# The first norm's inputs, factors and splits, re-ordered in a two-block model kernel

## What is computed

```python
def rms_norm(x, g):
    xf = x.astype(jnp.float32)
    y = xf * lax.rsqrt(jnp.mean(xf * xf, axis=-1, keepdims=True) + EPS)
    return (y * g.astype(jnp.float32)).astype(x.dtype)

def swiglu(x, w_gu, w_down):
    gate, up = jnp.split(x @ w_gu, 2, axis=-1)
    return (jax.nn.silu(gate) * up) @ w_down
```

## Time and profile before

| | us |
|---|---|
| median of 3 runs | 1676.66 |
| lowest and highest | 1675.67, 1677.74 |
| span of the profiled execution | 1677.2 |
| TensorE busy | 1640.7 (98%) |
| VectorE busy | 1189.8 (71%) |
| ScalarE busy | 878.0 (52%) |
| GpSimd busy | 51.2 (3%) |

### The profile page before, as it was taken

The page is one execution under the profiler, slowest core; times in us unless marked ns, Lnnn a source line. Parts: engine busy times, 40 slices in busy tenths (PEclk is TensorE's granted clock), DMA queues, the critical chain, the costliest instruction groups (busy, mean ns, idle before and its releaser), DMA issues.

```text
span 1677.2 us, 24153 instructions
## 1 busy us (share of the span) xinstructions
PE 1640.7 (98%) x9644; PEld 1425.4 (85%) x9644; DVE 1189.8 (71%) x1991; ACT 878.0 (52%) x1521; POOL 51.2 (3%) x87
## 2 busy tenths in 40 slices
PE   8999999999999999999999999999999999999997
PEld 7888899778888888889888888888888998888886
DVE  6766658957666776675877676786667887676777
ACT  5544456755444444455755444655444666454445
POOL 0000000001000000001210000000000000000000
PEclk9999999999999999999999999999999999999999
DMA  9545356034555455545345555545554443565541
GB/s 368 193 186 190 137 188 240 5 135 176 188 188 189 176 204 190 194 160 223 141 171 204 192 193 180 216 184 188 188 189 182 151 145 126 198 222 189 189 163 50
DMA packets 32111, 301.54 MB, mean 180 GB/s; under 512 B 3824, under 2 KB 4352, under 8 KB 6016
## 3 DMA queue, kind: packets, MB, share of 16 engines
q1 hardware_dynamic: 32000, 300.01, 48.6%
HBM read 298.93 MB, written 1.06 MB: 179 GB/s over the span
## 4 chain that ended last, share of the span: by engine, by line
PE 87%; DVE 7%; ACT 3%; issue 1%; POOL 0%; DMA 0%; SPq 0%; DVEq 0%; ACTq 0%
PE bank L477 28%; PE bank L467 27%; PE bank L466 12%; PE bank L456 9%; PE bank L469 2%; DVE w_lo L429 1%; PE bank L507 1%; PE bank L2087 1%; PE bank L580 1%; DVE x L848 1%; PE bank L581 1%; PE bank L605 1%; PE bank L2089 1%; PE bank L584 1%; PE bank L1684 1%
## 5 line engine op out<-in xcount | busy, mean ns | idle before, releaser
L429 DVE TENSOR_TENSOR w_lo<-w_raw,w_hi 128x1024 fp32r<-128x1024 f32 (+4 forms) x539 | 586.9, 1139 | 190.8 <-ACT w_hi L422 190.3
L467 PE MATMUL bank<-xT,w_hi 128*128 128x512 f32 x1920 | 673.8, 396 | 0.3 <-DVE w_lo L429 0.3
L422 ACT ACTIVATE w_hi<-w_raw 128x1024 fp32r<-128x1024 f32 (+5 forms) x543 | 500.3, 981 | 98.0 <-PE bank L477 82.1
L466 PE MATMUL bank<-xT,w_lo 128*128 128x256 f32 x1680 | 468.4, 279 | 0.0
L467 PEld LDWEIGHTS bank<-xT,w_hi 128*128 128x128 f32 x1920 | 351.6, 188 | 69.9 <-DVE w_lo L429 0.5
L466 PEld LDWEIGHTS bank<-xT,w_lo 128*128 128x128 f32 x1680 | 316.7, 189 | 10.4
L795 ACT ACTIVATE ff_silu<-ff_silu 128x256 f32<-128x256 f32 x124 | 51.9, 418 | 387.8 <-DVE ff_silu L948 387.8
L477 PE MATMUL bank<-w_hi,hT_hi 128*128 128x512 f32 x480 | 187.5, 391 | 0.0
L477 PE MATMUL bank<-w_hi,hT_lo 128*128 128x512 f32 x480 | 186.8, 389 | 0.0
L477 PE MATMUL bank<-w_lo,hT_hi 128*128 128x512 f32 x480 | 186.8, 389 | 0.0
L948 DVE TENSOR_REDUCE ff_silu<-bank 128x256 f32<-128x512 f32 x124 | 85.7, 691 | 101.7 <-PE bank L467 100.6
(11 more groups left out here) (398 smaller groups left out, 2170.4 us busy)
## 6 DMA issues: line engine op xcount, KB each, us to landing
w_raw<-in_ffn_a SPq DMA_DIRECT2D x22, 1536.0 KB, 6.6
w_raw<-in_ffn_b SPq DMA_DIRECT2D x22, 1536.0 KB, 6.4
w_raw<-in_ffn_c SPq DMA_DIRECT2D x22, 1536.0 KB, 6.5
w_raw<-in_ffn_d SPq DMA_DIRECT2D x22, 1536.0 KB, 6.6
w_raw<-in_ffn_e SPq DMA_DIRECT2D x22, 1536.0 KB, 6.5
w_raw<-in_ffn_f SPq DMA_DIRECT2D x22, 1536.0 KB, 6.4
gains<-in_gains SPq DMA_DIRECT2D x11, 1024.0 KB, 5.0
w_raw<-in_mla_up SPq DMA_DIRECT2D x8, 1280.0 KB, 5.8
```

The source lines that it names most:

```text
L422: nc.scalar.activation(hi, src, ACTF.Copy).then_inc(w_hi_made, 1)
L429: nc.vector.tensor_tensor(lo, src, hi.bitcast(F32), ALU.subtract).then_inc(w_lo_made, 1)
L466: nc.tensor.matmul(o[:, 0:SEQ], lo[:, c], xT[:, k, 0, :], start=False, stop=False)
L467: ins = nc.tensor.matmul(o, hi[:, c], xT[:, k, :, :], start=(k == 0), stop=(k == KD - 1))
```

## The change

- SP issues token block 0 first, then the identity, then the factors as one row on one partition (4 KB in place of 512 KB). Token block 1 is issued by ACT, as its first instruction.
- A row of 128 ones is written by POOL. TensorE multiplies it with the factor row, two fp32 products of 512 columns into PSUM banks 0 and 1 (`pe_spread_gains`), as the first thing on TensorE and so ahead of the 12 warming matmuls. `dve_rms_apply` reads the factors of this norm from PSUM.
- The first weight chunk comes in two transfers, 1024 columns with a semaphore of its own, and the other 2048.
- DVE does all four applications ahead of splits and low parts. ACT puts a split between turn 0 and turn 1. The low part of piece 3 goes from DVE to POOL, between the two roots of norm 0 and norm 1.

```diff
-        by_pool = 4 if (name, i) == ("ffn_b", 0) else 0
+        by_pool = {("ffn_a", 0): (3,), ("ffn_b", 0): (0, 1, 2, 3)}.get((name, i), ())
...
+            if i == 0 and b <= GU // 2:
+                act.wait_ge(w_front_landed, 16)
+            else:
+                act.wait_ge(w_landed[c.slot], c.landed)
...
+        def pe_spread_gains():
+
+            pe.wait_ge(ones_row_made, 1)
+            pe.wait_ge(gains_landed, 16)
+            for half in range(2):
+                ins = nc.tensor.matmul(psum[half][:, :], ones_row, gains[0:1, half_of(half)], start=True, stop=True)
+            ins.then_inc(gains_spread, 1)
...
-            dve.wait_ge(gains_landed, 16 * (n + 1))
+            gain = gains[:, c]
+            if n == 0:
+                dve.wait_ge(gains_spread, 1)
+                gain = psum[c.start // 512][:, :]
+            else:
+                dve.wait_ge(gains_landed, 16 * (n + 1))
             dve.wait_ge(rooted, 2 * n + b + 1)
...
             apply(0, 1, half_of(0))
-            dve_low(0, 0)
             apply(0, 0, half_of(1))
-            dve_low(0, 1)
             apply(0, 1, half_of(1))
             dve_split(first["ffn_a"], 0, 2)
+            dve_low(0, 0)
+            dve_low(0, 1)
+            dve_split(first["ffn_a"], 2, 3)
             dve_low(0, 2)
-            dve_split(first["ffn_a"], 2, 4)
             dve_low(0, 3)
...
+                at = 0
+                if i == 0:
+                    at = GU // 2
+                    nc.sync.dma_start(raw[c.slot][:, 0:at], c.source[:, 0:at]).then_inc(w_front_landed, 16)
+                nc.sync.dma_start(raw[c.slot][:, at:c.cols], c.source[:, at:c.cols]).then_inc(w_landed[c.slot], 16)
...
+            nc.sync.dma_start(x[:, 0, :], t["x"][tok_of(0), :]).then_inc(x_landed[0], 16)
             nc.sync.dma_start(const[:, 0:P], t["const"][:, 0:P]).then_inc(ident_landed, 16)
-            for b in range(TB):
-                nc.sync.dma_start(x[:, b, :], t["x"][tok_of(b), :]).then_inc(x_landed[b], 16)
-            nc.sync.dma_start(gains[:, 0:D], t["gains"][0:1, 0:D].to_broadcast([P, D])).then_inc(gains_landed, 16)
+            nc.sync.dma_start(gains[0:1, 0:D], t["gains"][0:1, 0:D]).then_inc(gains_landed, 16)
...
         def pe_program():
+            pe_spread_gains()
             pe.wait_ge(ident_landed, 16)
...
         def act_program():
+            nc.scalar.dma_start(x[:, 1, :], t["x"][tok_of(1), :]).then_inc(x_landed[1], 16)
             act_squares(0, x, False)
-            act_turn(0, (0, 1))
-            act_split(first["ffn_a"], 0, 2)
+            act_turn(0, (0,))
+            act_split(first["ffn_a"], 0, 1)
+            act_turn(0, (1,))
+            act_split(first["ffn_a"], 1, 2)
             act_turn(0, (2,))
...
         def pool_program():
+            nc.gpsimd.memset(ones_row, 1.0).then_inc(ones_row_made, 1)
             nc.gpsimd.memset(expo[:, :], -0.5).then_inc(minus_half_made, 1)
             pool_root(0)
+            split_lo_pool(first["ffn_a"])
             pool_root(1)
```

More of the change, by code:

```diff
@@ L231, in weight_stream @@
         hi += 1
-        if j < c.by_pool:
+        if j in c.by_pool:
             pool += 1
@@ L266, in build @@
         chunks, first, place = weight_stream(t)
+        w_front_landed = sem("w_front_landed")
         w_landed = [sem(f"w_landed_{i}") for i in range(RAW_SLOTS)]
@@ L283, in build @@
         minus_half_made, mean_made = sem("minus_half_made"), sem("mean_made")
+        ones_row_made, gains_spread = sem("ones_row_made"), sem("gains_spread")
         gate_up_made, gate_summed, silu_made, h_made, h_hi_made, h_lo_made, down_made = (
@@ L332, in build @@
         ident = cst("ident")
+        ones_row = sig[1][0:1, 0:P]
         def half_of(h):
@@ L403, in split_hi @@
             a, b = c.pieces[piece]
-            act.wait_ge(w_landed[c.slot], c.landed)
+            if i == 0 and b <= GU // 2:
+                act.wait_ge(w_front_landed, 16)
+            else:
+                act.wait_ge(w_landed[c.slot], c.landed)
             if is_held(c, piece):
@@ L432, in split_lo_pool @@
             c = chunks[i]
-            for piece in range(c.by_pool):
+            for piece in c.by_pool:
                 a, b = c.pieces[piece]
@@ L858, in dve_rms_apply @@
         def dve_rms_apply(n, b, c, dst):
-            dve.wait_ge(gains_landed, 16 * (n + 1))
+            gain = gains[:, c]
[4 more added lines that the diff above has]
+                dve.wait_ge(gains_landed, 16 * (n + 1))
             dve.wait_ge(rooted, 2 * n + b + 1)
-            nc.vector.scalar_tensor_tensor(dst[:, b, c], x[:, b, c], rstd[:, b:b + 1], gains[:, c],
+            nc.vector.scalar_tensor_tensor(dst[:, b, c], x[:, b, c], rstd[:, b:b + 1], gain,
                                            ALU.mult, ALU.mult).then_inc(normed, 1)
@@ L2446, in load @@
                         wait_split(sp, left)
-                nc.sync.dma_start(raw[c.slot][:, 0:c.cols], c.source).then_inc(w_landed[c.slot], 16)
+                at = 0
[3 more added lines that the diff above has]
+                nc.sync.dma_start(raw[c.slot][:, at:c.cols], c.source[:, at:c.cols]).then_inc(w_landed[c.slot], 16)
             def loads(a, b):
```

## The result

| | median, us | runs | lowest to highest |
|---|---|---|---|
| before | 1677.38 | 18 | 1675.03 to 1679.30 |
| changed | 1680.06 | 18 | 1678.52 to 1682.16 |

The ratio of changed to before is 1.0019, 95% interval 1.0013 to 1.0026: 2.2 to 4.4 us slower. The forecast was -0.5 us, and the range ended at 1678.6. These times are 1.3 us above the span of the same execution (the profiled one took 1679.42 and its span is 1678.1). So the span of the kernel before, 1677.2, should not have been set beside a median of times: by the same 1.3 the profiled execution of the kernel before took about 1678.5 (an estimate), 1.1 us above the median of 18. The two profiled spans are only 0.9 us apart; the last part of the account comes back to this.

What follows compares the result with a forecast made beforehand. TensorE, busy 1640.7 of 1677.2 us, was taken as the bound, so only the head could change the time. The first product moving -0.5 us and the rest 0 gave 1676.2 against 1676.66; range 1674.2 to 1678.6.

Steps and rivals of the forecast that it cites:

- Inputs: Head, token loads: block 0 lands at 4.6 or 5.4, and the application's wait for factors goes, 1.0 to 1.8 us.
- the nearer row: Token block 0's transfer: 4.7 us, as the second block took with two under way together, landing at 5.4.
- rival of two queues: Head transfers: queues share engines, factors land at 6.0, F is 16.15; +0.1 us, 1676.8; chance 0.15.
- The spread: Two fp32 factor products on TensorE: an added wait, 3.5 us from the factors' landing at 5.4, done at 8.9.
- The warm-up: 12 matmuls on TensorE, between spread and transposes: moved onto the path, taking 2.9 us.
- X: Start of the first transposes on TensorE: 9.58 before, forecast 11.8, 2.2 later.
- From X to F: Transposes to first product: the part gained, F = X + 3.75 in place of 6.44 between them.
- F: Start of the first product on TensorE: 16.02 before, forecast 15.5, 0.5 earlier.
- After F: First product to second chunk: no loss but no slack; TensorE wants the second chunk's pieces at F + 6.0.
- The sum: Whole kernel: F moves by -0.5 us, the rest by 0; 1676.2 against the median of 1676.66.
- late-clock rival: Warm-up on TensorE: clock rises only after its 24 instructions, 5.3 us, F 17.95; +1.9, 1678.6; chance 0.16.

Runs made afterwards that it cites:

- e5: The changed kernel without the spread: factors come repeated on 128 partitions and are read from SBUF; 1676.05 us, ratio 0.9993 to the kernel before.
- e2: The changed kernel with the identity issued first and the 12 warming matmuls ahead of the spread; 1677.20 us, ratio 1.0005 to the kernel before.
- e3: The changed kernel with the spread's products over 128 rows, 127 of them zero, instead of one; 1676.87 us, ratio 1.0004 to the kernel before.
- e8: The changed kernel with a 128-row spread, no 12 warming matmuls, all low parts on DVE, a signal per factor half; 1674.51 us, ratio 0.9987.
- e9: The kernel before with 22 warming matmuls of piece 0 in place of 12; 1677.66 us, ratio 0.9998.
- e4: The changed kernel with the low part of piece 3 back on DVE; run once, 1681.23 us, no ratio.
- e1: The changed kernel without its 12 warming matmuls of piece 0; 1678.08 us, ratio 1.0003 to the kernel before.
- e6: The kernel before with only the factor row, its spread on TensorE and the reading from PSUM; 1681.40 us, ratio 1.0022.

## Why the prediction was wrong, point by point

- **Inputs.** Block 0: 4.7 us from issue, landed at 5.4, as taken from the nearer row. Factors: forecast 5.4, measured 5.73. The rival of two queues was right in its mechanism (identity 4.65 us in e5, tokens at 6.3 in e2), but in the changed kernel it was hidden behind the warm-up.
- **The spread.** Forecast 3.5 us at the slow pace, done at 8.9; measured 3.75, done near 9.6. The pace was right.
- **The warm-up is the step that failed.** It was rightly put on the path, as what makes the faster factors useless. Its size was wrong: "the spread is as long as that, so I take the rise for done soon after its end and 2.9 us in all." It took 4.9, and e3 and the table of rises show why: one-row products did nothing towards the rise. The forecast took being busy for the cause, where the trace of before has only work over 128 rows ahead of the rise. So X was 14.33, not 11.8. With 128 rows the warm-up takes 2.92 in e3, the very figure forecast, but that match is partly luck. The rise 2.9 us after TensorE began, on which the forecast built, is the earliest of the eight executions that began with 128 rows; the others took 4.1 us and more. With the rise of e8, 6.1 us after the start, the warm-up of e3 would have taken some 3.8 us (an estimate from the two paces, 0.213 and 0.112).
- **From X to F.** Forecast X + 3.75, measured 18.07 - 14.33 = 3.74. Its terms held to 0.15 us. Against the 6.44 of the kernel before this is a gain of 2.7, of which 1.5 is the order and 1.2 the fast transposes: e9, with the old order and fast transposes, takes 5.23.
- **After F.** Forecast no loss. Measured 6.19 from F to the second chunk, where it was 5.99 by the chain and 5.83 by the timeline. The 0.2 to 0.4 is POOL's piece: in e4 it is 5.87 by the timeline.
- **The sum.** 2.05 to F and 0.2 to 0.4 behind it make 2.25 to 2.4, against 2.7 between the medians, 3.2 by the ratio, and 1.9 to 2.8 for the late-clock rival. That rival, X = 14.2 and F = 17.95 for 0.16 of the chance, is what happened, to 0.1 us. It was held to be chance; with one-row products ahead the rise was late in all four executions seen, the changed kernel, e1, e4 and e6. The range was set from 1676.66, the median of three runs, and 18 gave 1677.38; the rival's +1.9 would have been 1679.3.
- **The profiled executions.** Their spans differ by 0.9 us, not 2.25. Something far from the change works the other way. In the stretch 299 to 312 the granted clock was 0.74 before and 0.87 after:

```profile
299.00:312.00 13.00, 10.35 (x51) 8.32 (x51) 12.39 (x53) 9.73 (x37) 0.81 (x2) 0.74 0.01 2
```

```profile
299.00:312.00 13.00, 10.23 (x61) 7.63 (x60) 12.69 (x49) 9.99 (x39) 0.55 (x1) 0.87 0.01 2
```

The first row is the kernel before, the second the changed one. A mean of 0.74 over 13 us is 6.8 us at 1.2 GHz, one of 0.87 is 3.4 us. So the changed kernel was spared up to 1.7 us there, in code that the change does not touch. That is enough for the 1.35 us between 2.25 and the 0.9 seen, though it is not shown that all of it lies there. Over the runs of the kernel before, the mean granted clock goes from 0.997 to 0.993 as the time goes from 1674 to 1679. One pair of spans can't size an effect of 2 us here.

What stays open: the medians differ by 2.7 us, by the ratio it is 3.2, and the head by 2.25 to 2.4. Executions in which the clock rises later than in the one profiled would explain it. e4, whose TensorE does the same up to there, is such a one (rise at 15.0, X at 14.81), but how often it happens was not seen. Contractions of other sizes than one row and 128 were not tried. How much of the 1.5 us is the order on DVE, and how much ACT's, was not separated either.

## What to carry to other kernels

Before a step is put on an idle engine, look at what already stands in that engine's list behind it: cover that was free while the engine had nothing to do goes onto the path when a wait is put ahead of it. Ask of work that is to keep or raise TensorE's clock not whether the engine is busy but whether the trace shows this kind of work ahead of a rise; a row spread by one-row products looked busy and was not enough, and 127 rows of zeros repaired it. And where parts of a change are independent, time them apart: the new order alone was worth 1.5 to 2 us, and the spread hid it.

## What the runs showed of the hardware

- Two fp32 products of 512 columns over one row, 3.7 us of TensorE work, left the pace at 0.20 us per 128-column instruction for another 4.2 us; behind the same over 128 rows it was 0.112 after 0.4 us in e3 and after 2.4 us in e8.
- The pace doubled 2.9 to some 6 us after the first product in the executions that began with products over 128 rows, and 7.9 to 10.3 us after it in the four that began with one row.
- Small transfers took longer beside a fresh one on a second queue: the 64 KB identity took 1.9 us from issue in the kernel before, 3.8 in e2 (issued first, beside ACT's block) and 4.65 in e5 (behind block 0 as well).
- A 128x512 subtraction from SBUF took 1.61 us on DVE while POOL did one of 1.31 us, and 0.69 otherwise (changed kernel, and e3 and e5 to 0.01 us; 1.75 in e2).
- The clock column can print 1.00 where the pace of instructions is that of 1.2 GHz, at the start of the execution; the spacing of instructions showed it in every kernel here.
